# Last residual and final norm with tokens on partitions, and the last four down tiles bank by bank

## The reference

```python
x_lat = x_lat + mod_lat[5] * f_lat.reshape(bsz, seq, d)   # f_lat: output of the last PEER
return _rmsnorm(x_lat, final_gain)
```

## Time and profile before

| | us |
|---|---|
| median of 3 runs | 1851.7 (1850.59 to 1851.9) |
| profiled execution, its own time | 1850.75 |
| its span, first to last instruction | 1848.9 |
| PE busy | 1829.7 (99%) |
| DVE busy | 1509.6 (82%) |
| ACT busy | 965.7 (52%) |
| POOL busy | 451.1 (24%) |
| data moved | 376.34 MB, mean 204 GB/s |

### The profile page before, as it was taken

The page is one execution under the profiler, slowest core; times in us unless marked ns, Lnnn a source line. Parts: engine busy times, 40 slices in busy tenths (PEclk is TensorE's granted clock), DMA queues, the critical chain, the costliest instruction groups (busy, mean ns, idle before and its releaser), DMA issues.

```text
span 1848.9 us, 35387 instructions
## 1 busy us (share of the span) xinstructions
PE 1829.7 (99%) x11712; PEld 1586.2 (86%) x11712; DVE 1509.6 (82%) x2803; ACT 965.7 (52%) x1616; POOL 451.1 (24%) x225
## 2 busy tenths in 40 slices
PE   8999999999999999999999999999999999999998
PEld 7899988888888888888889998888888888888887
DVE  5775889979998888888888589987998888885555
ACT  6654455655555444444555545565555544444454
POOL 6046588950000000000000358893000000000000
PEclk9999999999999999999999999999999999999999
DMA  9866455556655555588874545555655555555553
GB/s 383 319 230 223 168 183 183 192 193 216 205 171 170 176 175 172 172 313 317 329 262 146 166 161 190 184 187 203 214 192 170 174 175 172 172 170 193 193 192 135
DMA packets 104178, 376.34 MB, mean 204 GB/s; under 512 B 12464, under 2 KB 12464, under 8 KB 103856
## 3 DMA queue, kind: packets, MB, share of 16 engines
q1 hardware_dynamic: 103392, 373.37, 58.9%
q0 software_dynamic: 432, 2.10, 0.3%
q10 hardware_dynamic: 288, 0.06, 0.0%
HBM read 374.43 MB, written 1.05 MB: 203 GB/s over the span
## 4 chain that ended last, share of the span: by engine, by line
PE 85%; DVE 3%; DMA 3%; POOL 3%; issue 2%; ACT 1%; SPq 1%; POOLq 0%; DVEq 0%; ACTq 0%
PE ring L1828 20%; PE O L1884 13%; PE O L1886 13%; PE O L1885 12%; PE ring L1831 10%; POOL wL L515 3%; PE ring L1542 2%; PE ring L1544 2%; PE ring L1543 2%; PE ring L1800 2%; PE ring L1821 2%; DMA raw<-in_u 1%; PE O L1821 1%; ACT wH L555 1%; PE ring L1802 1%
## 5 line engine op out<-in xcount | busy, mean ns | idle before, releaser
L555 ACT ACTIVATE wH<-raw 128x1024 fp32r<-128x1024 f32 x597 | 633.4, 1061 | 803.6 <-DMA raw<-in_v 367.2
L927 DVE TENSOR_TENSOR wL<-raw,wH 128x1024 fp32r<-128x1024 f32 x384 | 470.2, 1224 | 175.2 <-ACT wH L555 172.0
L1828 PE MATMUL ring<-hX,wH 128*128 128x512 f32 x1984 | 503.1, 396 | 0.5 <-POOL wL L515 0.5
L1828 PEld LDWEIGHTS ring<-hX,wH 128*128 128x128 f32 x1984 | 356.4, 189 | 64.6 <-POOL wL L515 0.9
L1884 PE MATMUL O<-wH,gateH 128*128 128x512 f32 x1024 | 405.3, 396 | 0.0
L1886 PE MATMUL O<-wH,gateL 128*128 128x512 f32 x1024 | 399.7, 390 | 0.0
L1885 PE MATMUL O<-wL,gateH 128*128 128x512 f32 x1024 | 398.6, 389 | 0.0
L515 POOL TENSOR_TENSOR wL<-raw,wH 128x1024 fp32r<-128x1024 f32 x128 | 321.0, 2515 | 48.0 <-ACT wH L555 46.4
L1831 PEld LDWEIGHTS ring<-hX,wL 128*128 128x128 f32 x1984 | 270.8, 190 | 19.6
L1831 PE MATMUL ring<-hX,wL 128*128 128x256 f32 x1984 | 276.4, 282 | 0.0
L1886 PEld LDWEIGHTS O<-wH,gateL 128*128 128x128 f32 x1024 | 192.2, 188 | 41.4
(11 more groups left out here) (217 smaller groups left out, 2340.8 us busy)
## 6 DMA issues: line engine op xcount, KB each, us to landing
raw<-in_u SPq DMA_DIRECT2D x256, 512.0 KB, 3.3
raw<-in_v SPq DMA_DIRECT2D x256, 512.0 KB, 3.3
ada_v<-in_ada SPq DMA_DIRECT2D x40, 512.0 KB, 4.4
raw<-in_w_q SPq DMA_DIRECT2D x30, 512.0 KB, 3.3
ada_m<-in_ada SPq DMA_DIRECT2D x24, 512.0 KB, 5.2
raw<-in_w_in SPq DMA_DIRECT2D x23, 512.0 KB, 4.1
ada_f<-in_ada SPq DMA_DIRECT2D x16, 512.0 KB, 15.1
raw<-in_w_out SPq DMA_DIRECT2D x16, 512.0 KB, 3.4
```

The lines of the kernel that those rows point to most:

```text
L555: nc.scalar.activation(wH[s % RAW][:, :], (place or raw[s % RAW])[:, :], ACT.Copy).then_inc(s_h, 1)
L927: nc.vector.tensor_tensor(wL[s % RAW][:, :], raw[s % RAW][:, :], wH[s % RAW][:, :].bitcast(fp32), ALU.subtract).then_inc(s_low, 1)
L1828: mm(bank[:, :], wH[s][:, k * P:k * P + P], hX[:, k, :, :].rearrange("p two t -> p (two t)"), start=(k == 0), stop=False)
```

## The change

The last sub-layer of layer 1 is finished with tokens on the partitions, so that the banks `O` need not be turned.

- PE: the down tiles 120 to 123 of layer 1 are each followed by four transposes of blocks of `XT` into a ring bank, so that `ring[b]` holds the residual stream in the layout of `O[b]`. The tiles 124 to 127 are worked as 16 pieces of tile and bank (three matmuls each, `value_part`) in the order `END_ORDER`, which finishes bank 0 after ten pieces, 1 after eleven, 2 after twelve and 3 at the end. PE has nothing after that.
- POOL: from tile 100 on it writes the column of gates (1024 values, `modcol(1, 5)`) to memory, loads the gains as rows (the host now gives them repeated for all partitions, 512 KB), and reads the gates back as a row repeated for all partitions. Later it multiplies three pieces by their gains.
- DVE: a bank at a time (bank 3 in two halves) `weighed = O * gate_row` and `otok = ring + weighed`; the sums of squares, the reciprocals, and the last scaling of bank 3.
- ACT: the squares of each piece with a sum along the row, two roots, and the scaling of the three pieces that POOL multiplied. The table load for the root (`warm_root`, L591) stands behind the high part of tile 127 in place of ahead of it.
- SP: three stores in place of four, with tokens on the partitions; the host turns the result.
- Layer 0 keeps its order; its semaphore counts are written without the layer.

```diff
             sb("under_otok", [P, 88 * T], at=oo)
             otok = sb("otok", [P, TT, D], at=oo)
+        with ExitStack() as end:
+            sb("under_end", [P, 64 * T], at=end)
+            gate_row = sb("gate_row", [P, D], at=end)
+            gain_row = sb("gain_row", [P, D], at=end)
+            weighed = sb("weighed", [P, TT, D], at=end)
+            squares = sb("squares", [P, TT, D], at=end)
+            sb("under_y", [P, 8 * T], at=end)
+            gained = sb("gained", [P, TT, D], at=end)
...
 
         bias_loads = [(adab[:, :], adab_d), (n1[:, :], n1_d)]
-        small_loads = [(n2[:, :], n2_d), (fg[:, :], fg_d), (vg[:, :], vg_d), (ps[:, :], ps_d), (bs[:, :, :], bs_d),
+        small_loads = [(n2[:, :], n2_d), (vg[:, :], vg_d), (ps[:, :], ps_d), (bs[:, :, :], bs_d),
                        (ws[:, :, :], ws_d)]
         BIAS, SMALL = 16 * len(bias_loads), 16 * len(small_loads)
-        NORMS = 2 * LAYERS + 1
+        GATED_FREE = EXP_TILES + 100
+        END_PIECES = ((0, 0, HALF), (1, 0, HALF), (2, 0, HALF), (3, 0, T), (3, T, HALF))
+        END_ORDER = ((0, 0), (0, 1), (1, 0), (1, 1), (0, 2), (2, 0), (2, 1), (1, 2), (2, 2), (3, 0), (3, 1), (3, 2),
+                     (0, 3), (1, 3), (2, 3), (3, 3))
+
+        def piece(tile, n):
+            b, lo, hi = END_PIECES[n]
+            at = b % 2 * HALF
+            return tile[:, b // 2, at + lo:at + hi]
+
+        def row_piece(row, n):
+            b, lo, hi = END_PIECES[n]
+            at = b % 2 * HALF
+            return row[:, at + lo:at + hi]
+
...
                     for s in range(4):
                         load(src, base, i, s)
-            for p in range(4):
-                sp.wait_ge(s_hf, p + 1)
-                sp.dma_start(out_d[:, 2 * p:2 * p + 2, :], hf[:, 2 * p:2 * p + 2, :]).then_inc(s_out, 16)
-            sp.wait_ge(s_out, 64)
+            sp.wait_ge(s_y_a, 2)
+            sp.dma_start(out_d[:, 0, :], otok[:, 0, :]).then_inc(s_out, 16)
+            sp.wait_ge(s_y_v, 1)
+            sp.dma_start(out_d[:, 1, HALF:], otok[:, 1, HALF:]).then_inc(s_out, 16)
+            sp.wait_ge(s_y_a, 3)
+            sp.dma_start(out_d[:, 1, 0:HALF], otok[:, 1, 0:HALF]).then_inc(s_out, 16)
+            sp.wait_ge(s_out, 48)
...
                     pool.wait_ge(s_pe, BASE["v", 0] + 116)
                     pool.dma_start(keys[:, 0], k1_d[1]).then_inc(s_late, 16)
                     pool.dma_start(keys[:, 1], k2_d[1]).then_inc(s_late, 16)
+                else:
+                    pool.wait_ge(s_gL2, GATED_FREE)
+                    pool.dma_start(gates_d.rearrange("j p -> p j"), modcol(1, 5), allow_slow_non_contiguous=True)\
+                        .then_inc(s_rows, 16)
+                    pool.dma_start(gain_row[:, :], fg_d).then_inc(s_rows, 16)
+                    pool.wait_ge(s_rows, 32)
+                    pool.dma_start(gate_row[:, :], gates_d.rearrange("j p -> (j p)").partition_broadcast(P)).then_inc(s_rows, 16)
+                    pool.wait_ge(s_rows, 48)
+                    for b in range(3):
+                        pool.wait_ge(s_joined, b + 1)
+                        nc.gpsimd.tensor_tensor(piece(gained, b), piece(otok, b), row_piece(gain_row, b), ALU.mult)\
+                            .then_inc(s_gained, 1)
...
@@ -875,23 +921,55 @@
                 with act.Fori(last + 1, 31) as i:
                     for s in range(4):
                         ahead_gated(i, s)
-                warm_root()
+                if layer < LAYERS - 1:
+                    warm_root()
                 ahead_gated(31, 0)
                 if layer < LAYERS - 1:
                     for s in (1, 2):
                         ahead(base, 31, s)
-
-                act.wait_ge(s_half, layer + 1)
-                for tt in range(TT):
-                    nc.scalar.activation(otok[:, tt, 0:512], O[2 * tt][:, :], ACT.Copy).then_inc(s_oc_a, 1)
-                act.wait_ge(s_pe, base + EXP_TILES)
-                nc.scalar.activation(otok[:, 1, 512:1024], O[3][:, :], ACT.Copy).then_inc(s_oc_a, 1)
-                for j in range(KT):
-                    act.wait_ge(s_res, KT * layer + j + 1)
-                    square(j)
-                if layer < LAYERS - 1:
+                    act.wait_ge(s_half, 1)
+                    for tt in range(TT):
+                        nc.scalar.activation(otok[:, tt, 0:512], O[2 * tt][:, :], ACT.Copy).then_inc(s_oc_a, 1)
+                    act.wait_ge(s_pe, base + EXP_TILES)
+                    nc.scalar.activation(otok[:, 1, 512:1024], O[3][:, :], ACT.Copy).then_inc(s_oc_a, 1)
+                    for j in range(KT):
+                        act.wait_ge(s_res, j + 1)
+                        square(j)
                     ahead(base, 31, 3)
-                norm(2 * layer + 2)
+                    norm(2 * layer + 2)
+                else:
+                    def sum_squares(n):
+
+                        act.wait_ge(s_joined, n + 1)
+                        nc.scalar.activation(piece(squares, n), piece(otok, n), ACT.Square,
+                                             accum_out=square_sum[:, n:n + 1]).then_inc(s_squared, 1)
+
+                    def end_root(tt, n):
+
+                        act.wait_ge(s_squared, n + 1)
+                        act.wait_ge(s_rest, tt + 1)
+                        nc.scalar.activation(std[:, tt:tt + 1], square_sum[:, n:n + 1], ACT.Sqrt,
+                                             bias=rest[:, 2 * tt:2 * tt + 1], scale=1.0 / D).then_inc(s_end_std, 1)
+
+                    def end_scaled(n, tt):
+
+                        act.wait_ge(s_gained, n + 1)
+                        act.wait_ge(s_end_inv, tt + 1)
+                        act.wait_ge(s_squared, n + 1)
+                        nc.scalar.activation(piece(otok, n), piece(gained, n), ACT.Copy, scale=inv[:, tt:tt + 1])\
+                            .then_inc(s_y_a, 1)
+
+                    warm_root()
+                    sum_squares(0)
+                    sum_squares(1)
+                    end_root(0, 1)
+                    sum_squares(2)
+                    end_scaled(0, 0)
+                    sum_squares(3)
+                    end_scaled(1, 0)
+                    sum_squares(4)
+                    end_root(1, 4)
+                    end_scaled(2, 1)
...
             def norm(n):
                 inverse_root(n)
                 dve.wait_ge(s_rstd, n + 1)
-                if n == NORMS - 1:
-                    for k in range(KT):
-                        ins = nc.vector.scalar_tensor_tensor(hf[:, k, :], XT[:, k, :], fg[:, k:k + 1], O[2][:, 0:T], ALU.mult,
-                                                             ALU.mult)
-                        if k % 2:
-                            ins.then_inc(s_hf, 1)
-                    return
                 scaled(n, 0)
                 scaled(n, 1)
                 for k in range(KT):
...
                     modulations(6, 11, (2, 3))
 
-                dve.wait_ge(s_pe, base + EXP_TILES)
-                nc.vector.tensor_copy(otok[:, 0, 512:1024], O[1][:, :]).then_inc(s_oc_v, 1)
-                for j in range(KT):
-                    if j % 2 == 0:
-                        dve.wait_ge(s_ot, layer * 4 + j // 2 + 1)
-                    residual(layer, 5, j, ring[j // 2], j % 2).then_inc(s_res, 1)
-                norm(2 * layer + 2)
+                if layer == 0:
+                    dve.wait_ge(s_pe, base + EXP_TILES)
+                    nc.vector.tensor_copy(otok[:, 0, 512:1024], O[1][:, :]).then_inc(s_oc_v, 1)
+                    for j in range(KT):
+                        if j % 2 == 0:
+                            dve.wait_ge(s_ot, j // 2 + 1)
+                        residual(layer, 5, j, ring[j // 2], j % 2).then_inc(s_res, 1)
+                    norm(2)
+                else:
+                    def weigh(n):
+
+                        b, lo, hi = END_PIECES[n]
+                        dve.wait_ge(s_bank_done, b + 1)
+                        return step(nc.vector.tensor_tensor(piece(weighed, n), O[b][:, lo:hi], row_piece(gate_row, n),
+                                                            ALU.mult))
+
+                    def join(n):
+
+                        b, lo, hi = END_PIECES[n]
+                        nc.vector.tensor_tensor(piece(otok, n), ring[b][:, lo:hi], piece(weighed, n), ALU.add)\
+                            .then_inc(s_joined, 1)
+
+                    def partial(tt, n):
+
+                        dve.wait_ge(s_squared, n + 1)
+                        return nc.vector.tensor_scalar(rest[:, tt:tt + 1], square_sum[:, n:n + 1], 1.0 / D, EPS,
+                                                       ALU.mult, ALU.add)
+
+                    def end_inverse(tt):
+
+                        dve.wait_ge(s_end_std, tt + 1)
+                        nc.vector.reciprocal(inv[:, tt:tt + 1], std[:, tt:tt + 1]).then_inc(s_end_inv, 1)
+
+                    dve.wait_ge(s_rows, 48)
+                    dve.wait_ge(s_ot, 8)
```

(63 more changed lines are left out.)

27 lines of the change are left out of this document (17 added, 10 removed).

## The result

The changed kernel takes 1862.08 us (median of 5 runs, 1861.67 to 1863.81) against 1851.70 for the kernel before: ratio 1.0054 [1.0043, 1.0065], 10 us slower. Forecast were 1848.8 and a range up to 1850.9. The result lies on the side of rival E, to which I had given 7%, and 3.7 us beyond its 1858.4.

The account below looks back on a forecast made before the run. The prediction took PE's matmul count to bound the kernel until 1836 us, then a serial tail of 12.41 us. Its terms, 1.9 + 0 - 4.8 + 0 = -2.9 us, took 1851.7 to 1848.8; range 1847.2 to 1850.9.

Parts of the forecast that it names:

- rival E: Around tile 100: the 1024 four-byte elements block the DMA engines, PE idles 9.6 us, total 1858.4 us; chance 0.07.
- part 4: From tile 100 of layer 1's down projection: POOL's three DMAs for gates and gains cost 0 us.
- the megabyte runs beside the stream: From tile 100: POOL's two 512 KB loads, gains and gates, run alongside the tile loads and cost 0 us.
- Transposes among the tiles: Tiles 120 to 123: sixteen residual transposes on a full PE cost 1.9 us, bounds 1.75 to 2.7.
- Due dates of the last tiles: Tiles 124 to 127 bank by bank: loads wanted earlier but still in time, cost 0 us, bounds 0 and 0.8.
- rival C: End tiles: PE starves on tile 127 or 126, idling 0.2 to 0.8 us, total 1850.4 us; chance 0.12.
- The tail: After PE's last product: 7.6 us to the span's end against 12.4, a gain of 4.8; bounds 6.9 to 8.6.
- DVE's wait of 0.8 behind the third join: In the tail: DVE waits some 0.8 us for ACT's square of piece 2 before weighing bank 3.
- POOL's products: In the ending: POOL's three multiplications by gains, 1.3 to 1.8 us each for 512 columns, stay hidden.
- rival D: In the ending: DVE's joins 1 and 2 wait for POOL's products, 1.6 us less gained, total 1850.4 us; chance 0.04.
- the exemption for one input in PSUM: In the ending: DVE operations with at most one SBUF input don't contend with POOL, so weighing and joining are free.
- Layer 0 and the start untouched: Layer 0 keeps its order, so no change was expected until 1750 us.

Follow-up runs that it names:

- store_32_bytes: The changed kernel with the gate column stored as it lies, 128 elements of 32 bytes, wrong output: 1850.78 us, ratio 0.9995.
- store_spread: The changed kernel with the gate column's store split into eight DMAs of 128 four-byte elements, two tiles apart from tile 84: 1871.46 us, ratio 1.0106.
- store_in_before: The kernel before with only POOL's store of the gate column added at tile 100 of layer 1, result unread: 1861.32 us, ratio 1.0053.
- turned_no_xt: turned_by_pe without the 16 transposes of the residual stream in tiles 120 to 123, wrong output: 1851.05 us, ratio 0.9993.
- no_store: The changed kernel without the gate column's store, the gate row loaded from the gains' array instead, wrong gates: 1850.94 us, ratio 0.9993.
- turned_by_pe: The changed kernel with the gate column turned by one PE transpose at tile 64 and stored as 8 rows of 512 bytes: 1851.18 us, ratio 0.9997.

## Why the prediction was wrong, by its steps

The step that failed is part 4, "The 1024 small elements have no row; see rival E for its upper bound. I take 0, since 128 elements of 32 bytes landed in 1.9". The row taken was a load, of elements of another size; the thing to be priced was a store of 4-byte neighbours. It measured 12.2 us (10.6 of gap and 1.6 of clock). store_32_bytes shows how well that row fitted its own kind (2.7 us, no gap) and how little it said on the other. With it the overlap was wrong: "the megabyte runs beside the stream" holds only for the megabyte.

Rival E named the place, the waiting tile load and PE's gap rightly and priced it at 9.6. Its mechanism was wrong though its sum was near, which is luck: it had each element occupy its engine like a row of 4 KB. But store_spread, with an eighth of the elements in each DMA, was worse, and in store_in_before the store's packets are all recorded in 2 us, and the slow time comes behind them. E also left out the clock. It was given 7% on the ground that "queues take turns on an engine, so the stream still gets its share"; from 1758 to 1764 the stream's queue had 2 packets of 53. The upper bound of E stood in the rivals but not in the range, which ended at 1850.9. With an upper bound of 1858 on an operation of a kind that the trace had never shown, 7% was too little.

The other steps:
- Transposes among the tiles, 1.9 (1.75 to 2.7): 1.8 by the timeline, 1.9 from products of store_32_bytes less before (177.23 - 175.32). Right.
- Due dates of the last tiles, 0.3 to spare for tile 127 and 0.8 for 126, charged 0: no gap there in the changed kernel or in any that has the transposes. The argument against rival C, a landing of 3.5 at most, is weaker than it looked: in turned_no_xt the load of tile 126 took 4.2, and other traces have up to 5.0 a few tiles earlier.
- The tail, 7.6 (6.9 to 8.6) in place of 12.4: 8.1. The steps up to DVE's last result are within 0.1 (it ends at 4.94, forecast 4.84); ACT's last scaling ends at 4.96, forecast 4.7, since a scaling took 0.71 and not 0.60. The terms that were short: the start of the last store's issue, 5.36 and forecast 5.22, and 2.7 from there to the end in place of 2.4 (that issue took 0.43, not 0.35, and the landing 2.3).
- DVE's wait of 0.8 behind the third join: 0.72. POOL's products: 3.90 for three, 1.3 each, and DVE's joins kept 0.69, so rival D is out, and the exemption for one input in PSUM, on which the prediction drew, holds here.
- The megabyte beside the stream at 0: a gap of 0.9 in no_store, none in store_32_bytes and turned_by_pe.
- Layer 0 and the start untouched: nothing shows otherwise, but executions differ by 1 to 3 us there, and less than that can't be seen.

What stays open: why the tile loads get nearly nothing while such a store is on its way; where between 4 and 32 bytes a store of neighbours stops being slow, and whether it is the length of an element or the distance that counts there (4-byte elements 32 bytes apart were not run); and how a gap varies from run to run, since each kernel has one trace.

## What to carry to other kernels

A DMA has to be priced by its pattern in memory too, not by its bytes or its count alone: a store of 4 KB in 4-byte neighbours from different partitions cost 12 us in a kernel whose whole new ending gains 2.3. Look for stretches in which loads are on their way and only some 35 GB/s are moved; the busy share of the DMA engines doesn't show them, it was 0.92 in one such stretch and 0.23 in another. Before a column is turned by a DMA, turn it on PE (one transpose, and a store of rows of 512 bytes): here that took the loss of 10 us back to the level of the kernel before.
When a moved operation shortens a chain, look at what then arrives together: here three stores, and giving the first its own early slot was worth 0.6 us.

## What the runs showed of the hardware

- Stores from SBUF to memory on POOL's queue, beside the tile loads, us to landing: 128 elements of 4 bytes side by side 7.5 to 12.5 (nine stores), at 64 or 512 bytes 2.6 and 2.5; 1024 of 4 bytes side by side in rows of 128 9.8 to 12.1 (four stores), 1024 at 64 bytes 4.0; 128 elements of 32 bytes side by side 2.7; 8 rows of 512 bytes 2.6.
- While a slow one is on its way, all queues together move 32 to 39 GB/s, at a busy share of the engines of 0.92 (changed kernel, a load of POOL's queue outstanding) or of 0.23 and 0.32 (store_in_before). A tile load of 512 KB on the other queue that takes 3.3 takes up to 16.0 in the first and 11.2 in the second.
- After a gap of 10.6 us PE came back at 1.2 GHz and made seven steps, the first of 0.59 us and the others of 0.43, before 2.4 GHz was granted again.
